# A mixture-of-experts kernel on Trainium2: a quarter of the last expert's second down tile moved from SyncE's queue to GpSimd's, in four strips of eight partitions

## The chip, the cores and the metric

The kernel runs on one core of one Trainium2 chip. The metric is device time in microseconds of one execution; the kernel before takes 1707.98 us (median of 3 runs, 1707.73 to 1708.21).

## The reference

The kernel computes a two-layer transformer block stack and then a second block whose last part is a mixture-of-experts feed-forward. Only that last part matters here: 272 tokens of width 1024, 16 experts, each of which takes its 34 best tokens (2 * 272 / 16).

```python
logits = jnp.einsum('ld,de->le', hs, w_router)
aff = jax.nn.softmax(logits, axis=-1)
g, idx = lax.top_k(aff.T, cap)
xg = hs[idx]
a = jnp.einsum('ecd,edf->ecf', xg, w_gate)
u = jnp.einsum('ecd,edf->ecf', xg, w_up)
y = jnp.einsum('ecf,efd->ecd', jax.nn.silu(a) * u, w_down)
y = y * g[..., None]
out = jnp.zeros((L, D)).at[idx.reshape(-1)].add(y.reshape(-1, D))
```

The result is added to the stream, normalised (RMS) and the last 256 tokens are the output. All weights are float32. An expert has a gate and an up matrix of 1024 x 2048 and a down matrix of 2048 x 1024: 24 MB, read once from device memory.

## The kernel before, in words

All five engines run one straight program each; semaphores tie them together. Weights come through a ring of six places of 2 MB (`RING_T`: 128 partitions of 4096 float32, that is 16 KB a partition). `LOADS` lists the tiles in the order in which they take the places; SyncE (SP) walks that order and issues one transfer a tile, or one of 4 MB for two neighbouring places (`pair_ring`, L3423). Before a transfer SP waits on `w.prev.left`, the semaphore that TensorE raises when it has left the tile that lay in that place before. The transfer raises the semaphore of the place (`w.sem`) by 16 when all of it has landed.

An expert `e` has twelve tiles: `("g", e, i)`, `("u", e, i)` and `("d", e, i)` for i = 0 to 3. TensorE (PE) takes them in `gate_up(e, i)` (the matmuls of L1417 and L1418, gate into partitions 0 to 33 of a PSUM bank, up into 64 to 97) and `down(e, i, u)` (L1444 and L1445, four steps `c` of 128 rows of the down matrix each, left and right half of the output). Each step shows as two rows a line, so `down` of a tile has eight rows of L1444. Between them `turn_hidden` transposes the hidden values (L1429).

The last expert (e = 15) is cut finer, so that its last tiles can be used while they arrive. In SP's order its last tiles are: `("g", 15, 3)` (L3420), `("u", 15, 3)` in two halves (L3452), `("d", 15, 0)` and `("d", 15, 1)` whole (L3420), `("d", 15, 2)` in two halves and `("d", 15, 3)` in four quarters (L3463). PE waits for the whole of `("d", 15, 1)` on `w.sem`; for the pieces of the last two tiles it waits on `last0` to `last5`.

After the last matmul of `down` ScalarE and VectorE copy the expert's output (L3146), PE adds it to the stream (L1480), the norm follows on VectorE and ScalarE (L3152 to L3176, L2199 to L2212), and SP stores the output in four transfers (L3467, L3469).

GpSimd (POOL) has 39 instructions in the whole program. Its part in the experts is `pool_experts` (L3267 on): two memsets, one of `Y`, one of `OG`, and three multiplications that weigh the one-hot routing map. After them its program ends. It issues no transfer. `WK`, which the change writes to, is a scratch tile of the routing that nobody reads after the first expert.

Of the kernel before, what the change touches and what calls it, by code (L numbers as in the profile page):

```python
# [20 lines left out]
SLOT = 4096  # L21
# [3 lines left out]
E_N = 16  # L25
# [76 lines left out]
PIECES["d", 0, 0] = (0, 2, 4, 8)  # L102
PIECES_OF = {y: len(PIECES[x]) - 1 for tiles, x in REFILLS for y in tiles}
PIECES_OF.update({("g", 0, 2): 4, ("u", 0, 2): 4})

BESIDE = {("g", 1, 3): 3, ("u", 1, 3): 2, ("d", 1, 0): 4}
BESIDE.update({("g", 2, 1): 3, ("u", 2, 1): 2, ("g", 2, 2): 4, ("g", 3, 0): 3, ("u", 3, 0): 2, ("g", 3, 1): 4})
# [182 lines left out]
def bc(ap, *shape):  # L290
# [15 lines left out]

    "split_hi", "split_lo", "dhh", "dhl", "rooted", "rooted_t", "cxs", "lam_d", "dcos", "drope", "amax", "asoft", "osq", "osub", "onorm", "czero", "conv",

    "routed", "sel", "wkzero", "rscaled", "rmax", "rexp", "raff", "rtop", "rmask", "rank", "above", "onehot", "ogzero", "og", "yzero", "esilu", "edown", "fin_in", "fin_rs", "fin_root", "weighed", "final_d", "final_a",
]  # L310


# [968 lines left out]
def pe_experts(nc, k):  # L1281
# [150 lines left out]
    def down(e, i, u):  # L1432
        w = k.weight_at("d", e, i)
        pieces = e == E_N - 1 and i >= 2
        if not pieces:
            pe.wait_ge(w.sem, w.n)
        t = P["eturn", e, i]
        pe.wait_ge(t.taken, t.done)
        for c in range(4):
            if pieces and (i == 3 or c % 2 == 0):  # L1440
                pe.wait_ge(s[f"last{c // 2 if i == 2 else 2 + c}"], 16)
            hs = v.HD[e % 2][:, 4 * i + c, :]
            first, end = i == 0 and c == 0, i == 3 and c == 3
            pe.matmul(u.t[0:CAP, :], hs, w.v(4, 1024)[:, c, 0:512], start=first, stop=end)  # L1444
            ins = pe.matmul(u.t[64:64 + CAP, :], hs, w.v(4, 1024)[:, c, 512:1024], start=first, stop=end)  # L1445
            if 2 * c + 2 in PIECES.get(("d", e, i), ())[1:-1]:
                ins.then_inc(s["first_used"], 1)
        if i < 3:
            ins.then_inc(s["edown"], 1)
            w.left = (s["edown"], 3 * e + i + 1)  # L1450
        else:
            ins.then_inc(u.full, 1)
            w.left = (u.full, u.n)
# [1814 lines left out]
def pool_experts(nc, k):  # L3268
    pool, s, v, P = nc.gpsimd, k.sem, k.ex, k.banks
    pool.wait_ge(P["rms", "ffn2"].full, P["rms", "ffn2"].n)  # L3270
    pool.memset(v.WK[0:16, 0:6], 2.0).then_inc(s["wkzero"], 1)
    pool.memset(v.mx, 0.0).then_inc(s["wkzero"], 1)

    u = P["egu", 0, 3]
    pool.wait_ge(u.full, u.n)
    pool.memset(v.Y[32:64, :, :], 0.0).then_inc(s["yzero"], 1)
    pool.wait_ge(s["yzero"], 1)
    pool.memset(v.OG.rearrange("p a b -> p (a b)"), 0.0).then_inc(s["ogzero"], 1)
    pool.wait_ge(s["onehot"], 6)
    pool.wait_ge(s["ogzero"], 1)  # L3280
    for i, (r, m) in enumerate(TILES):
        o = v.OH[0:m, i, :].rearrange("p (e s) -> p e s", s=CAP)
        af = v.AFF[0:m, i, :].rearrange("p (e a) -> p e a", a=1).to_broadcast([m, E_N, CAP])
        pool.tensor_tensor(v.OG[0:m, i, :].rearrange("p (e s) -> p e s", s=64)[:, :, 0:CAP], o, af, ALU.mult).then_inc(s["og"], 1)


def gpsimd_program(nc, k):
# [17 lines left out]
def sync_program(nc, k):  # L3305
    sp, s, A, P = nc.sync, k.sem, k.A, k.banks
# [58 lines left out]
    def part(x, e, i):  # L3365

        if x == "d":
            return A["w_down_2"][e, i // 2][:, SLOT * (i % 2):SLOT * (i % 2 + 1)]
        return A["w_gate_up_2"][e, i][:, SLOT * (x == "u"):SLOT * (x == "u") + SLOT]
# [52 lines left out]
    def pair_ring(x, e, i):  # L3422

        head, tail = k.ring[x, e, i], k.ring[("u", e, i) if x == "g" else ("d", e, i + 1)]
        sp.wait_ge(*head.prev.left)
        sp.wait_ge(*tail.prev.left)
        src = A["w_gate_up_2"][e, i] if x == "g" else A["w_down_2"][e, i // 2]
        sp.dma_start(flat(k.ring.pair((x, e, i))), src).then_inc(head.sem, 16)

    heads = set(PAIRED.values())  # L3430
    for e in range(E_N):
        if e:
            for i in range(4):
                for x in "gu":
                    if (x, e, i) in heads:
                        pair_ring(x, e, i)
                    elif (x, e, i) in PAIRED:
                        continue
                    elif (x, e, i) not in PIECES_OF and (x, e, i) != ("u", E_N - 1, 3):
                        beside_ring(x, e, i)  # L3440
        if e == 5:

            sp.wait_ge(*k.first["g", 3, 0].left)
            sp.dma_start(k.CB[:, :], A["fin"].broadcast_to([128, D])).then_inc(s["fin_in"], 16)
        if e == E_N - 1:


            w = k.ring["u", e, 3]
            sp.wait_ge(*w.prev.left)
            for c in range(2):  # L3450
                a, b = 2 * D * c, 2 * D * (c + 1)
                sp.dma_start(w.t[:, a:b], part("u", e, 3)[:, a:b]).then_inc(s[f"lastu{c}"], 16)  # L3452
        for i in range(4):
            if ("d", e, i) in heads:
                pair_ring("d", e, i)
            elif e and (e < E_N - 1 or i < 2) and ("d", e, i) not in PIECES_OF and ("d", e, i) not in PAIRED:
                beside_ring("d", e, i)
    for i, n, first in ((2, 2, 0), (3, 4, 2)):
# [131 lines left out]
```

## Time and profile before

| | us |
|---|---|
| median of 3 runs | 1707.98 |
| the profiled execution's own time | 1706.41 |
| its span, first to last instruction | 1704.7 |
| TensorE busy | 1608.2 (94%) |
| VectorE busy | 734.9 (43%) |
| ScalarE busy | 472.3 (28%) |
| GpSimd busy | 33.6 (2%) |

The profile is of one execution. TensorE's granted clock is 0.98 of full speed over the span. In the experts' part, from about 870 us on, the 16 DMA engines are busy throughout and move some 432 GB/s. The chain of work that ended last has PE in 70% of the span and DMA in 25%. The profiled execution's own time is 1.7 us above its span.

### The profile page before, as it was taken

The numbers are of one execution on the slowest core, as the hardware profiler recorded it, in microseconds if no ns is written. First come the engines' busy times: TensorE is split into PE (matmuls) and PEld (weight loads), VectorE is DVE, ScalarE is ACT, GpSimd is POOL, SyncE is SP. The second block draws the span as 40 slices with busy tenths as digits, with TensorE's granted clock in tenths as the row PEclk, the third lists the DMA queues.
The fourth block names the chain that finished last, engine by engine and source line by source line (L and its number), as shares of the span: only waits on it lengthen the run. The fifth ranks groups of instructions, "written<-read, shape, count | busy, mean of one in ns | idle before, by whom it ended". The sixth has DMA issues, their size and how long they took to land.

```text
span 1704.7 us, 22917 instructions
## 1 busy us (share of the span) xinstructions
PE 1608.2 (94%) x9593; PEld 980.0 (57%) x9593; DVE 734.9 (43%) x1462; ACT 472.3 (28%) x839; POOL 33.6 (2%) x39
## 2 busy tenths in 40 slices
PE   7999999999999999999999989889889889889998
PEld 5777999998999999787322322323223223223332
DVE  3778888878886557885111101101101101111102
ACT  3537634348653337743000000000000000000001
POOL 0100000000000001100100000000000000000000
PEclk9999999999999999999999999999999999999999
DMA  9964479891466454249999999999999999999997
GB/s 390 374 245 194 187 308 355 322 356 60 189 255 227 170 219 152 107 169 384 421 399 431 430 436 432 431 433 432 432 433 431 432 432 431 434 433 431 431 428 298
DMA packets 37972, 577.69 MB, mean 339 GB/s; under 512 B 4304, under 2 KB 5360, under 8 KB 9584
## 3 DMA queue, kind: packets, MB, share of 16 engines
q1 hardware_dynamic: 37872, 576.24, 81.7%
q8 instruction: 77, 1.26, 0.3%
q14 instruction: 23, 0.19, 0.0%
HBM read 575.17 MB, written 1.05 MB: 338 GB/s over the span
## 4 chain that ended last, share of the span: by engine, by line
PE 70%; DMA 25%; DVE 2%; issue 1%; ACT 1%; SPq 0%; DVEq 0%; ACTq 0%
DMA RING_T<-in_w_gate_up 23%; PE P L1417 17%; PE P L1444 6%; PE P L991 5%; PE P L993 5%; PE P L992 5%; PE P L595 4%; PE P L1009 2%; PE P L1008 2%; PE P L1010 2%; PE P L604 2%; PE P L1375 1%; DMA RING_T<-in_w_down 1%; PE P L1179 1%; PE P L1181 1%
## 5 line engine op out<-in xcount | busy, mean ns | idle before, releaser
L1417 PE MATMUL P<-RING_T,SCR 128*34 128x512 f32 x928 | 429.5, 618 | 62.4 <-DMA RING_T<-in_w_gate_up 57.2
L1418 PE MATMUL P<-RING_T,SCR 128*34 128x512 f32 x960 | 444.5, 618 | 0.0
L1417 PEld LDWEIGHTS P<-RING_T,SCR 128*34 128x34 f32 x928 | 102.5, 115 | 337.1 <-issue 317.3
L3105 DVE TENSOR_TENSOR SCR<-P,SCR 34x512 f32<-34x512 f32 x64 | 44.4, 693 | 500.6 <-ACT SCR L2169 500.5
L1444 PE MATMUL P<-RING_T,SCR 128*34 128x512 f32 x480 | 222.0, 612 | 14.9 <-issue 14.0
L1445 PE MATMUL P<-RING_T,SCR 128*34 128x512 f32 x480 | 222.3, 612 | 0.0
L2169 ACT ACTIVATE SCR<-P 34x512 f32<-34x512 f32 x64 | 37.6, 588 | 543.7 <-PE P L1418 543.7
L993 PE MATMUL P<-SCF 128*128 128x256 f32 x640 | 181.1, 283 | 0.0
L991 PE MATMUL P<-SCF 128*128 128x256 f32 x640 | 181.1, 283 | 0.0
L992 PE MATMUL P<-SCF 128*128 128x256 f32 x640 | 181.1, 283 | 0.0
L1444 PEld LDWEIGHTS P<-RING_T,SCR 128*34 128x34 f32 x480 | 51.2, 114 | 148.7 <-issue 144.2
L991 PEld LDWEIGHTS P<-SCF 128*128 128x128 f32 x640 | 122.9, 192 | 0.0
L993 PEld LDWEIGHTS P<-SCF 128*128 128x128 f32 x640 | 122.9, 192 | 0.0
L992 PEld LDWEIGHTS P<-SCF 128*128 128x128 f32 x640 | 122.9, 192 | 0.0
L2654 DVE TENSOR_TENSOR SCF<-RING_T,SCF 128x1024 fp32r<-128x1024 f32 x88 | 106.1, 1221 | 30.0 <-ACT SCF L1818 30.0
L1818 ACT ACTIVATE SCF<-RING_T 128x1024 fp32r<-128x1024 f32 x88 | 91.9, 1054 | 52.7 <-PE P L1010 27.9
L1418 PEld LDWEIGHTS P<-RING_T,SCR 128*34 128x34 f32 x960 | 106.0, 115 | 0.0
L1540 ACT ACTIVATE SCR<-P 128x256 f32<-128x256 f32 (+7 forms) x112 | 45.1, 417 | 199.5 <-PE P L1375 125.5
L1008 PE MATMUL P<-SCF 128*128 128x256 f32 x352 | 99.6, 283 | 0.0
L1009 PE MATMUL P<-SCF 128*128 128x256 f32 x352 | 99.6, 283 | 0.0
L1010 PE MATMUL P<-SCF 128*128 128x256 f32 x352 | 99.6, 283 | 0.0
L2327 DVE SCALAR_TENSOR_TENSOR RING_T<-RING_T,CB 128x1024 f32<-128x1024 f32 x80 | 93.1, 1220 | 9.0 <-DMA RING_T<-in_ada_w 4.8
(465 smaller groups left out, 2533.4 us busy)
## 6 DMA issues: line engine op xcount, KB each, us to landing
RING_T<-in_w_gate_up SPq DMA_DIRECT2D x47, 4096.0 KB, 20.5
RING_T<-in_w_down SPq DMA_DIRECT2D x22, 4096.0 KB, 21.6
RING_T<-in_ada_w SPq DMA_DIRECT2D x24, 2048.0 KB, 10.6
RING_T<-in_ffn_w SPq DMA_DIRECT2D x22, 2048.0 KB, 8.1
RING_T<-in_w_gate_up SPq DMA_DIRECT2D x15, 2048.0 KB, 19.0
RING_T<-in_ffn_w SPq DMA_DIRECT2D x22, 1024.0 KB, 6.6
RING_T<-in_w_down SPq DMA_DIRECT2D x11, 2048.0 KB, 18.4
RING_T<-in_ab_w_in SPq DMA_DIRECT2D x7, 2048.0 KB, 17.0
```

The lines of the kernel that those rows point to most:

```text
L991: pe.matmul(o, wh, v.HH[:, 0, c, :], start=c == 0, stop=False)
L992: pe.matmul(o, wh, v.HH[:, 1, c, :], start=False, stop=False)
L993: ins = pe.matmul(o, wl, v.HH[:, 0, c, :], start=False, stop=c == KC - 1)
L1008: pe.matmul(o, wh, v.HR[:, f % NHD, 0, :], start=f == 0 and m % 2 == 0, stop=False, skip_group_check=True)
L1009: pe.matmul(o, wh, v.HR[:, f % NHD, 1, :], start=False, stop=False, skip_group_check=True)
L1010: ins = pe.matmul(o, wl, v.HR[:, f % NHD, 0, :], start=False, stop=f == 21, skip_group_check=True)
L1417: pe.matmul(u.t[0:CAP, :], xs, wg.v(KC, 512)[:, c, :], start=c == 0, stop=c == KC - 1)
L1418: ins = pe.matmul(u.t[64:64 + CAP, :], xs, wu.v(KC, 512)[:, c, :], start=c == 0, stop=c == KC - 1)
L1444: pe.matmul(u.t[0:CAP, :], hs, w.v(4, 1024)[:, c, 0:512], start=first, stop=end)
L1445: ins = pe.matmul(u.t[64:64 + CAP, :], hs, w.v(4, 1024)[:, c, 512:1024], start=first, stop=end)
L2327: nc.vector.scalar_tensor_tensor(out=src, in0=src, scalar=1.0, in1=k.CB[:, :], op0=ALU.mult, op1=ALU.mult, accum_out=k.MOD[:, layer, 4 * i ...
L2654: nc.vector.tensor_tensor(lo, w.up()[:, :, z, j * 128:(j + 1) * 128], hi.bitcast(F32), ALU.subtract).then_inc(k.sem["lo"], 1)
```

## The change

One tile, `("d", 15, 1)`, is named `SHARED`. SP loads its partitions 0 to 95 as before. GpSimd, at the end of its program, waits for the same semaphore value as SP (`w.prev.left`), and then issues eight transfers: four times a tiny one (8 partitions of 8 float32 from the `c_cols` input into the scratch tile `WK`; nobody waits for it) and behind it eight partitions of the tile, every fourth one: 96, 100, ... 124, then 97, 101, ... 125, and so on. Each of these strips is 8 x 16 KB = 128 KB. PE waits for both the place's semaphore and for `shared` at 64 (four transfers of 16).

```diff
+SHARED = ("d", E_N - 1, 1)
...
+        if ("d", e, i) == SHARED:
+            pe.wait_ge(s["shared"], 64)
...
+    w, src = k.ring[SHARED], k.A["w_down_2"][SHARED[1], 0][:, SLOT:2 * SLOT]
+    pool.wait_ge(*w.prev.left)
+    for r in range(96, 100):
+        pool.dma_start(v.WK[0:8, 8 * (r - 96):8 * (r - 96) + 8], k.A["c_cols"][0:8, :]).then_inc(s["spare"], 16)
+        pool.dma_start(w.t[r:128:4, :], src[r:128:4, :]).then_inc(s["shared"], 16)
...
+            elif ("d", e, i) == SHARED:
+                w = k.ring[SHARED]
+                sp.wait_ge(*w.prev.left)
+                sp.dma_start(w.t[0:96, :], part("d", e, i)[0:96, :]).then_inc(w.sem, 16)
```

How it moves instructions, first on SP, at the end of the last expert. Before (`in_w_down` is the down matrix, `full4` and `full0` are raised by PE at the end of a `gate_up`):

```order
L3420 DMA RING_T<-in_w_gate_up 128x4096 [waits full1]
L3452 DMA RING_T<-in_w_gate_up 128x2048 [waits full1]
L3452 DMA RING_T<-in_w_gate_up 128x2048
L3420 DMA RING_T<-in_w_down 128x4096 [waits full4] x2
L3463 DMA RING_T<-in_w_down 128x2048 [waits full0]
L3463 DMA RING_T<-in_w_down 128x2048
```

And after the change, the same place:

```order
L3428 DMA RING_T<-in_w_gate_up 128x4096 [waits full1]
L3460 DMA RING_T<-in_w_gate_up 128x2048 [waits full1]
L3460 DMA RING_T<-in_w_gate_up 128x2048
L3428 DMA RING_T<-in_w_down 128x4096 [waits full4]
L3467 DMA RING_T<-in_w_down 96x4096 [waits full4]
L3475 DMA RING_T<-in_w_down 128x2048 [waits full0]
L3475 DMA RING_T<-in_w_down 128x2048
```

The second whole down tile has become one of 96 partitions; nothing else moved on SP.

On POOL, the end of its program after the change (before, it ends with the three multiplications):

```order
L3287 TENSOR_TENSOR SCR<-SCR 16x16x34
L3291 DMA SCR<-in_c_cols 8x8 [waits full4]
L3292 DMA RING_T<-in_w_down 8x4096
L3291 DMA SCR<-in_c_cols 8x8
L3292 DMA RING_T<-in_w_down 8x4096
L3291 DMA SCR<-in_c_cols 8x8
L3292 DMA RING_T<-in_w_down 8x4096
L3291 DMA SCR<-in_c_cols 8x8
L3292 DMA RING_T<-in_w_down 8x4096
```

Eight transfers stand behind one wait; nothing of POOL's is queued behind them.

On PE, the start of `down(15, 1)` after the change (before, the same row as L1444 waits for `taken1` and `weights3` alone):

```order
L1430 MATMUL P<-C,SCR 128x34 [waits taken4,taken1]
L1430 MATMUL P<-C,SCR 128x34 x3
L1447 MATMUL P<-RING_T,SCR 34x512 [waits taken1,shared,weights3]
L1448 MATMUL P<-RING_T,SCR 34x512
L1447 MATMUL P<-RING_T,SCR 34x512
```

One wait is added, in front of all the rest of PE's program.

## Rows read from the trace of the kernel before

**Rows 1.** The page: DMA busy and GB/s in 40 slices, and the chain by engine.

```profile
DMA  9964479891466454249999999999999999999997
GB/s 390 374 245 194 187 308 355 322 356 60 189 255 227 170 219 152 107 169 384 421 399 431 430 436 432 431 433 432 432 433 431 432 432 431 434 433 431 431 428 298
...
PE 70%; DMA 25%; DVE 2%; issue 1%; ACT 1%; SPq 0%; DVEq 0%; ACTq 0%
```

**Rows 2.** Chain that ended last, last 24 us: start us, us, what.

```profile
1670.40 0.39 PE P L1417
...
1673.13 19.89 DMA RING_T<-in_w_down
1693.02 0.04 issue
1693.06 0.62 PE P L1444
```

**Rows 3.** Stretches: length, busy of PE, PEld, DVE, ACT, POOL; PEclk; DMA share, GB/s.

```profile
1400.00:1600.00 200.00, 180.45 (x864) 60.09 (x864) 29.79 (x76) 12.64 (x24) 0.00 (x0) 0.96 1.00 432
...
1660.00:1685.00 25.00, 24.29 (x130) 8.83 (x128) 3.28 (x7) 3.05 (x4) 0.00 (x0) 1.00 0.99 421
...
1688.00:1689.00 1.00, 1.00 (x8) 0.35 (x6) 0.00 (x0) 0.00 (x0) 0.00 (x0) 1.00 0.52 213
1689.00:1690.00 1.00, 1.00 (x6) 0.24 (x4) 0.00 (x0) 0.00 (x0) 0.00 (x0) 1.00 0.50 205
1690.00:1691.00 1.00, 1.00 (x8) 0.34 (x6) 0.00 (x0) 0.00 (x0) 0.00 (x0) 1.00 0.40 164
1691.00:1692.00 1.00, 1.00 (x8) 0.16 (x6) 0.00 (x0) 0.00 (x0) 0.00 (x0) 1.00 0.27 111
1692.00:1693.00 1.00, 0.88 (x4) 0.00 (x0) 0.00 (x0) 0.00 (x0) 0.00 (x0) 1.00 0.15 53
```

**Rows 4.** Timeline of SP, last issues of weights: start us, us of issuing, line.

```profile
1652.82 0.91 SPq L3452 DMA_DIRECT2D RING_T<-in_w_gate_up  x2
1661.41 1.57 SPq L3420 DMA_DIRECT2D RING_T<-in_w_down  x2
1670.86 2.70 SPq L3463 DMA_DIRECT2D RING_T<-in_w_down  x6
```

**Rows 5.** Source L3420 from 1650 us (one gate, two down tiles): start and landing.

```profile
L3420 SPq DMA_DIRECT2D RING_T<-in_w_down x2: 328/760/1193, 1661.4 to 1661.8; - x2
...
DMA to landing us min/median/max: 16.0/16.8/21.3
```

**Rows 6.** Timeline of PE at the two whole down tiles.

```profile
1678.48 0.62 PE L1444 MATMUL P<-RING_T,SCR 128*34 128x512 f32 x1
...
1682.04 0.43 PE L1429 MATMUL P<-C,SCR 34*128 34x34 f32 x4
1683.14 0.62 PE L1444 MATMUL P<-RING_T,SCR 128*34 128x512 f32 x1 [0.67 <-DMA RING_T<-in_w_down]
```

**Rows 7.** Timeline of PE at the last step.

```profile
1692.28 0.59 PE L1444 MATMUL P<-RING_T,SCR 128*34 128x512 f32 x1
...
1693.06 0.62 PE L1444 MATMUL P<-RING_T,SCR 128*34 128x512 f32 x1 [0.18 <-DMA RING_T<-in_w_down]
```

**Rows 8.** Issues by line: KB each, median us from issue to landing.

```profile
RING_T<-in_w_down SPq DMA_DIRECT2D x2, 256.0 KB, 3.6
...
SCR<-in_c_cols SPq DMA_DIRECT2D x1, 4.0 KB, 1.6
```

**Rows 9.** Groups of instructions of POOL: busy us, mean ns of one.

```profile
L3278 POOL MEMSET SCR<- 128x3072 f32 x1 | 2.7, 2657 | 0.1
```

More of the change, by code:

```diff
@@ L307 @@
     "split_hi", "split_lo", "dhh", "dhl", "rooted", "rooted_t", "cxs", "lam_d", "dcos", "drope", "amax", "asoft", "osq", "osub", "onorm", "czero", "conv",
-    "routed", "sel", "wkzero", "rscaled", "rmax", "rexp", "raff", "rtop", "rmask", "rank", "above", "onehot", "ogzero", "og", "yzero", "esilu", "edown", "fin_in", "fin_rs", "fin_root", "weighed", "final_d", "final_a",
+    "routed", "sel", "wkzero", "rscaled", "rmax", "rexp", "raff", "rtop", "rmask", "rank", "above", "spare", "shared", "onehot", "ogzero", "og", "yzero", "esilu", "edown", "fin_in", "fin_rs", "fin_root", "weighed", "final_d", "final_a",
 ]
```

## The prediction

> **What bounds the kernel now.** I read the page first: from about 870 us on the DMA engines show 9 tenths in every slice and the rate stands at 431 to 436 GB/s [rows 1]. The chain of work is 70% PE and 25% DMA [rows 1], so the end of the experts' part is set by the stream of weights, with PE close behind. The chain's last pieces say who ends last: PE up to 1670.8 us, SP's six issues, then one transfer of 19.89 us that lands at 1693.02, and PE's last step from 1693.06 [rows 2]. Behind that step stand 1704.7 - 1693.06 = 11.6 us (copy, add, norm, store) that the change leaves alone.
>
> The stretches tell how the stream ends. Over 200 us the 16 engines move 432 GB/s at a share of 1.00 [rows 3]: 27.0 GB/s each, so one partition's row of 16,384 B takes an engine 0.607 us, and a tile of 128 rows is eight rows or 4.86 us an engine. But the engines do not finish together. From 1688 on the share is 0.52, 0.50, 0.40, 0.27, 0.15 [rows 3]: about half of them are done by 1688, and the others trail by 2 to 5 us. The work left after 1688 is 0.52 + 0.50 + 0.40 + 0.27 + 0.15 = 1.84 us of all 16 engines. Spread evenly it would end at 1689.8 and not at 1693.0. So there are up to 3.2 us in balancing the engines, and that is the whole stake of this change as a gain: 0.19% of the time. **A measurement of this kernel can tell some 0.2% (3.4 us) from no change.**
>
> How close PE is behind: `down(15, 0)` starts at 1678.48, its transposes end at 1682.47, and `down(15, 1)` starts at 1683.14 after 0.67 us of waiting [rows 6]. The last step waits only 0.18 us of idle by the profile, and its matmul follows the one before, which started at 1692.28, by 0.78 instead of the usual 0.43 us [rows 7]: some 0.35 us of waiting. So PE could end at most 0.67 + 0.35 = 1.02 us sooner, if weights came early enough from `("d", 15, 0)` on.
>
> **The change, part by part.**
>
> SP's transfer of the tile: 96 rows in place of 128, six rows an engine in place of eight. Each engine has 2 x 0.607 = 1.21 us less from SP. SP still issues one transfer, at 0.33 to 1.19 us [rows 5]; nothing gained or lost there, as the queue of the engines is 16.8 to 21.3 us deep at that time [rows 5] and hides it.
>
> GpSimd's four strips: 32 rows. The bytes are the same, so all engines together have the same 128 rows. What counts is on which engines the strips fall. A strip has eight rows of 16 KB, so it can keep at most eight engines busy with a row each. The trace of before has no transfer of eight partitions and no transfer from POOL, so I bound it from both sides. If the strips fall evenly, each engine gets 2 rows back: 0. If all four fall on the same eight engines, these have 6 + 4 = 10 rows (+1.21 us) and the other eight have 6 (-1.21 us). The Trainium skill ("DMA: Bandwidth & Descriptors", on why a DMA increments its semaphore by 16) says that GpSimd's transfer of eight rows takes eight engines that follow each other from a cursor that moves on; by that the tiny one takes one half and the strip always the other half, and the result would be one of the two outer values, never 0. No row here shows it.
>
> - On the eight engines that trail: their last landing moves from 1693.02 to 1694.23. The strips are issued from 1661.4 on and share the engines with what SP has queued, so up to 4 x 0.607 = 2.43 us are put ahead of `("d", 15, 0)`, which landed at 1661.41 + 16.8 = 1678.2 [rows 4, 5] and would land at 1680.6. PE starts there at 1680.7. From there PE needs 1682.47 - 1678.48 = 3.99 us to be ready for tile 1, and 1692.28 + 0.43 - 1683.14 = 9.57 us to the last step: 1694.26, when the last piece lands too. The last step starts at 1694.28 in place of 1693.06: **+1.2 us**.
> - On the eight that lead: they end at 1688 + 1.2 = 1689.2, still ahead of the rest. The trailing ones end at 1691.8. Tile 1 was issued at 1661.8, took 21.3 us [rows 5] and so landed at 1683.1; now it lands at 1681.9, before PE is ready. PE runs through from 1678.48: + 3.99 + 9.57 = 1692.04 for the last step, in place of 1693.06: **-1.0 us**.
>
> The tiny transfers: 8 x 32 B each. The nearest row is the transfer of 4 KB that lands in 1.6 us [rows 8]; its bytes are nothing to an engine (4 KB is a quarter of one 16 KB row, 0.15 us at most if all on one). Four of them: 0 to 0.6 us on one engine. I take 0, by the bytes.
>
> GpSimd's issuing: eight instructions behind a wait that ends with SP's, at 1661.4 [rows 4]. Nobody's work is queued behind them on POOL. It matters only if the last strip lands after PE wants it. That is 1683.1 before, and PE could be late to tile 1 by 0.35 us without moving the end. There is no row of an issue on POOL. Lower bound: SP's 0.33 us [rows 5], in all 2.6 us. Upper bound: POOL's longest instruction, 2.66 us [rows 9], in all 21.3 us. The strip itself needs about the 3.6 us of a transfer of 256 KB [rows 8]. Last strip landed: 1667.6 to 1686.3. I take the lower half, since issuing a transfer is no pass over 3072 elements a partition: inside the cover of 21.7 us, price 0, and +2.8 us at the upper end (1686.3 - 1683.1 - 0.35). VectorE is busy 3.28 us of the 25 us from 1660 to 1685 [rows 3]. If it held GpSimd up for all of it, that would still be inside the cover for any issue up to 1.8 us. The Trainium skill ("SBUF — State Buffer", on who interferes with whom) says that some VectorE operations lock GpSimd out while it writes the descriptors of a transfer; by that the strips come up to those 3.3 us later.
>
> PE's second wait: no instruction of its own in the order; if the strips are there, 0.
>
> **Sum and choice.** -1.0, 0 or +1.2 us by the place of the strips, and 0 to +2.8 from issuing. Nothing in the trace says which half trails. I take the trailing half (+1.2), for a reason of the bounds: everything else that the change adds (eight issues, four more transfers, one more wait, two queues that take turns on one engine) can only cost. The profiled execution took 1706.41 us, 1.57 below the median of 1707.98; 1706.41 + 1.2 = 1707.6 for such an execution, and against the median 1707.98 + 1.2 = **1709.2 us**.
>
> **The rivals.**
>
> *The strips fall on the leading half.* For it: the tail shows that half of the engines are free from 1688 [rows 3], and the four strips and tiny ones between them look made to pick one half. Against it: no row names the halves. Time: 1707.98 - 1.0 = 1707.0. Chance 0.30.
>
> *The strips bring no shift at all:* each falls on other engines, or what ends the stream is not the engine but the place in SBUF that it writes to, which has the same rows to take whoever brings them. For it: a share of 1.00 at 27.0 GB/s each [rows 3] fits both limits. Time: 1708.0. Chance 0.20.
>
> *GpSimd is late, and I am on the wrong side of 0.2%.* Mechanism: PE stands at `down(15, 1)` for the strips. It decides from the point at which the last strip lands after 1683.5; each us beyond is a us at the end. For +3.4 us the last strip must land at 1686.9, that is (1686.9 - 3.6 - 1661.4) / 8 = 2.7 us an issue. At 3.5 us an issue: 1661.4 + 28 + 3.6 = 1693.0, PE then has 9.57 us to the last step: 1702.6, +9.5 us, 1717.5. For it: GpSimd has issued no transfer before, and its first one may be slow. Against it: only its own longest instruction is as slow. Chance 0.10.
>
> The forecast (trailing half) has 0.40.
>
> **How the numbers follow.** The first three cases lie within 1707.0 to 1709.2, all closer to before than 3.4 us, together 0.90. The forecast case with issues at the upper bound would come to 1709.2 + 2.8 = 1712.0. Executions of before differ by 0.5 us among three. The range must hold 8 in 10: from 1706.4 (leading half, less the spread) to 1711.4 (trailing half, strips a little late). Faster by over 0.2% would need more than the whole stake of 3.2 us: 0.03. Slower by over 0.2%: nearly all of the late GpSimd, 0.09. Within: 0.88.
>
> **What would show it.** The stretches from 1688 on: if the trailing half got the strips, the shares after 1688 fall to zero one to one and a half us later than now and the lead ends about 1687; if the leading half, the 0.5 comes later and the zero sooner, near 1692. The timeline of PE at tile 1: a wait for `in_w_down` from POOL longer than 0.67 us would be the late GpSimd; no wait at all the leading half. In the issues by line, four transfers of 128 KB on POOL landing well before 1683 confirm the cover. I am wrong if the end moves by more than 3.4 us, if the stretches after 1688 look as before, or if something before 1661 us changes, where the change does nothing.

## The result, and the profile after

| | before | after |
|---|---|---|
| median of 4 runs each, same chip | 1707.95 us (1707.73 to 1708.21) | 1721.29 us (1719.24 to 1724.83) |
| profiled execution, its span | 1706.41 us, 1704.7 us | 1722.38 us, 1720.8 us |

The change makes the kernel slower: ratio 1.0083, 95% interval 1.0072 to 1.0095, or 13.3 us. The prediction said 1709.2 us, within 1706.4 to 1711.4. A few executions took 300 us or more longer, whatever the kernel (one of before at 2003.6 us, one of a variant at 3226.0 us), and the ratios leave them out.

The page of the changed kernel, DMA busy and GB/s in 40 slices, and the chain by engine, as [rows 1] of before:

```profile
DMA  9864479881566463349999999999999999999996
GB/s 392 356 246 198 186 309 362 319 345 54 215 232 237 152 247 147 119 180 395 415 402 430 433 433 433 431 433 431 434 430 435 432 430 430 433 431 431 433 396 183
...
PE 65%; DMA 30%; DVE 2%; issue 1%; ACT 1%; SPq 0%; DVEq 0%; ACTq 0%
```

The slices end with 396 and 183 in place of 428 and 298, and five per cent of the chain have gone from PE to DMA. The chain of before ended with a wait for SP's last piece [rows 2]. Here its last wait is the one for SP's 96 partitions of the cut tile: 36.22 us of DMA, up to 1699.54, and behind it PE runs through the rest of `down` without a wait. First the timelines of SP and POOL and the issues by line, then PE at the two whole down tiles, as [rows 4, 6, 8]:

```profile
1662.94 0.33 SPq L3428 DMA_DIRECT2D RING_T<-in_w_down  x1
1663.32 1.14 SPq L3467 DMA_DIRECT2D RING_T<-in_w_down  x1
1672.61 2.72 SPq L3475 DMA_DIRECT2D RING_T<-in_w_down  x6
```

```profile
1663.22 0.70 POOL L3291 DMA_DIRECT2D SCR<-in_c_cols  x1 [825.89 <-PE P L1419]
1663.91 0.52 POOL L3292 DMA_DIRECT2D RING_T<-in_w_down  x1
...
1666.98 0.52 POOL L3292 DMA_DIRECT2D RING_T<-in_w_down  x1
```

```profile
RING_T<-in_w_down SPq DMA_DIRECT2D x1, 1536.0 KB, 36.2
...
RING_T<-in_w_down POOLq DMA_DIRECT2D x4, 128.0 KB, 8.3
SCR<-in_c_cols POOLq DMA_DIRECT2D x4, 0.2 KB, 7.4
```

```profile
1685.30 0.43 PE L1430 MATMUL P<-C,SCR 34*128 34x34 f32 x4
1692.12 1.04 PE L1447 MATMUL P<-RING_T,SCR 128*34 128x512 f32 x1 [6.39 <-issue]
...
1698.46 0.43 PE L1430 MATMUL P<-C,SCR 34*128 34x34 f32 x4
1699.58 0.62 PE L1447 MATMUL P<-RING_T,SCR 128*34 128x512 f32 x1 [0.69 <-DMA RING_T<-in_w_down]
```

GpSimd is on time: eight issues of 0.52 to 0.70 us, and the strips land 8.3 us (median; 15.2 at most) after their issue, by 1666.98 + 15.2 = 1682.2 us. What is late is SP's own transfer of 96 partitions: it lands 36.2 us after its issue, at 1699.5, where the whole tile took 21.3 us [rows 5]. The tile ahead of it, `("d", 15, 0)`, is late too: PE stands 6.39 us for it, with the label "issue" since the profile names no releaser. The stretches say what the 16 engines did, as [rows 3]:

```profile
1400.00:1600.00 200.00, 180.69 (x868) 60.44 (x867) 28.95 (x74) 13.04 (x25) 0.00 (x0) 0.96 1.00 430
1660.00:1666.00 6.00, 5.74 (x38) 3.14 (x36) 0.99 (x2) 0.59 (x1) 2.78 (x6) 1.00 0.98 416
1666.00:1670.00 4.00, 4.00 (x22) 1.42 (x20) 0.00 (x0) 0.00 (x0) 1.50 (x3) 1.00 1.02 367
1670.00:1684.00 14.00, 10.33 (x45) 3.40 (x42) 0.99 (x2) 0.59 (x1) 0.00 (x0) 0.88 1.07 268
1684.00:1686.00 2.00, 1.73 (x12) 0.50 (x7) 0.00 (x0) 0.59 (x1) 0.00 (x0) 1.00 0.91 131
1686.00:1694.00 8.00, 1.88 (x6) 0.64 (x8) 0.99 (x2) 1.28 (x1) 0.00 (x0) 0.59 0.93 206
1694.00:1700.00 6.00, 5.31 (x20) 1.36 (x17) 0.30 (x1) 0.00 (x0) 0.00 (x0) 0.69 1.00 338
```

Read the last two columns together. From 1666 to 1694 the share stays between 0.91 and 1.07: in the mean the engines have a packet under way nearly all the time. Yet they move 367, 268, 131, 206 GB/s. Over these 28 us that is 4 x 367 + 14 x 268 + 2 x 131 + 8 x 206 = 7130, and 12,100 at 432: the missing 4970 are 11.5 us of the full stream. This execution is 1722.38 - 1706.41 = 16.0 us longer than the profiled one of before; 1.5 us of that were there before the change acts (SP issues the first down tile at 1662.94 and not at 1661.41), so 11.5 us stand against 14.5. The engines are not idle, their rows are slower: from 1670 to 1684 a row of 16,384 B takes 16 x 1.07 x 16,384 B / 268 GB/s = 1.05 us in the mean, in place of 0.607. That is what the experiments had to explain. PE's granted clock is 0.59 in the mean of 1686 to 1694, after PE has stood idle for 6.39 us, and its matmul at 1692.12 takes 1.04 us in place of 0.62. In this kernel that costs nothing, since PE then waits 0.69 us more for the tile that lands at 1699.5, and runs at full clock from there. In several of the experiments it does cost, and it is told there.

### The profile page after: what moved, and what is told of

Same layout as the page of the kernel before. It is cut to its first block, busy times and chain, and to the rows that moved or that the text cites. A ratio compares the mean times of both kernels' runs of the same rounds, so it can differ in the third digit from the quotient of the medians.

```text
span 1720.8 us, 22925 instructions
## 1 busy us (share of the span) xinstructions
PE 1603.4 (93%) x9593; PEld 982.1 (57%) x9593; DVE 734.8 (43%) x1462; ACT 472.4 (27%) x839; POOL 38.5 (2%) x47
## 3 DMA queue, kind: packets, MB, share of 16 engines
HBM read 575.17 MB, written 1.05 MB: 335 GB/s over the span
## 4 chain that ended last, share of the span: by engine, by line
PE 65%; DMA 30%; DVE 2%; issue 1%; ACT 1%; SPq 0%; DVEq 0%; ACTq 0%
DMA RING_T<-in_w_gate_up 28%; PE P L1418 14%; PE P L1447 5%; PE P L994 4%; PE P L992 4%; PE P L993 4%; PE P L596 4%; PE P L1010 2%; PE P L1009 2%; PE P L1011 2%; DMA RING_T<-in_w_down 2%; PE P L605 2%; PE P L1376 1%; PE P L1180 1%; PE P L1181 1%
## 5 line engine op out<-in xcount | busy, mean ns | idle before, releaser
L1418 PE MATMUL P<-RING_T,SCR 128*34 128x512 f32 x928 | 424.8, 612 | 67.6 <-DMA RING_T<-in_w_gate_up 63.9
```

The costliest lines, as they stand in the source:

```text
L1418: pe.matmul(u.t[0:CAP, :], xs, wg.v(KC, 512)[:, c, :], start=c == 0, stop=c == KC - 1)
```

## The experiments

All times of variants of the kernel stand beside runs of the kernel before on the same chip. The theories at the start, for where the loss comes from: the use of GpSimd's queue (A), the cut of the tile at partition 96 (B), the strips of eight rows (C). In the cuts of code, `...` stands for lines left out.

**1. The tiny transfers alone.** SP loads the whole tile, GpSimd issues only the tiny ones, PE waits for them.

```diff
-            pe.wait_ge(s["shared"], 64)
+            pe.wait_ge(s["spare"], 64)
...
-        pool.dma_start(w.t[r:128:4, :], src[r:128:4, :]).then_inc(s["shared"], 16)
...
-                sp.dma_start(w.t[0:96, :], part("d", e, i)[0:96, :]).then_inc(w.sem, 16)
+                sp.dma_start(w.t, part("d", e, i)[:, :]).then_inc(w.sem, 16)
```

> SyncE loads the whole second down tile again (128 partitions); GpSimd issues only the four tiny transfers behind the same wait, and TensorE waits for them at the second down tile. Theory A (the use of GpSimd's queue itself slows the engines): 1715 us or more, with GB/s under 320 in 1668 to 1695 us. Theory B (the cut of the tile over 96 partitions breaks the pairing of DMA engines and places in SBUF) and theory C (the strips of eight partitions share eight engines with SyncE's rows): 1708 us, stretches as before.

Measured: 1707.97 us beside 1707.59; ratio 1.0005 (0.9994 to 1.0016). A second queue, its issues and PE's second wait cost nothing that can be told.

**2. SP alone, 96 partitions and then 32.** Nothing on GpSimd: its wait and its eight transfers are left out, and PE waits for one transfer on `shared`.

```diff
                 sp.dma_start(w.t[0:96, :], part("d", e, i)[0:96, :]).then_inc(w.sem, 16)
+                sp.dma_start(w.t[96:128, :], part("d", e, i)[96:128, :]).then_inc(s["shared"], 16)
```

> No transfer from GpSimd. SyncE loads partitions 0 to 95 and then, in a transfer of its own, 96 to 127. Theory A and C: 1708 us (A: no second queue; C: no transfer of eight partitions). Theory B: 1714 us or more; the rate falls below 300 GB/s once the 96-partition transfer runs (from about 1678 us), and not before.

Measured: 1720.96 us, ratio 1.0081 (1.0052 to 1.0111), +13.4. A loss of the same size is there without any use of GpSimd; A falls, and C, which said 1708 us here, is not needed for it. Stretches of this kernel, and PE's start on the cut tile:

```profile
1666.00:1670.00 4.00, 4.00 (x22) 1.43 (x20) 0.00 (x0) 0.00 (x0) 0.00 (x0) 1.00 1.03 438
...
1672.00:1678.00 6.00, 6.00 (x30) 1.69 (x30) 0.99 (x2) 0.36 (x1) 0.00 (x0) 1.00 1.03 269
1678.00:1694.00 16.00, 8.36 (x30) 2.29 (x26) 1.29 (x3) 1.87 (x2) 0.00 (x0) 0.79 1.00 220
1694.00:1700.00 6.00, 4.26 (x11) 1.14 (x13) 0.00 (x0) 0.00 (x0) 0.00 (x0) 0.53 0.77 309
```

```profile
1695.74 1.03 PE L1447 MATMUL P<-RING_T,SCR 128*34 128x512 f32 x1 [3.75 <-issue]
```

The rate holds until 1672 us (418 GB/s from 1670 on), some 10 us after the cut tile's issue at 1661.7, and then falls to 269 and 220 GB/s. The fall comes 6 us sooner than expected.

Not all of this loss is the stream's. PE had stood idle for 5.63 and then 3.75 us before it started on the cut tile at 1695.74, its granted clock is 0.53 from 1694 to 1700, near the lower of its two levels (1.2 GHz), and seven steps of its matmuls take 5.7 us in place of 3.0 (0.82 to 0.86 us each for most of them, and not 0.43). PE has no wait behind that, so these 2.7 us go straight to the end. The profiled execution closes by this: the cut tile is started 1695.74 - 1683.14 [rows 6] = 12.6 us later than before, less the 0.35 us that PE waited at its last step [rows 7], plus 2.7, is 14.95; it took 1721.34 - 1706.41 = 14.93 us more. Experiments 3 and 4 have such slow steps too, 1.7 us each.

**3. SP alone, 96 partitions and the four strips.**

```diff
+                for r in range(96, 100):
+                    sp.dma_start(w.t[r:128:4, :], part("d", e, i)[r:128:4, :]).then_inc(s["shared"], 16)
```

> No transfer from GpSimd. SyncE loads partitions 0 to 95 and then the same four strips of eight partitions. Theory A: 1708 us. Theory B: as slow as the 96 and 32 cut. Theory C: slower than the 96 and 32 cut by the strips' 4 rows on eight engines, 1.2 to 2.4 us, and by more if sharing a place in SBUF is what costs.

Measured: 1718.66 us, ratio 1.0064 (1.0041 to 1.0088), +11.1: no worse than one transfer of 32. C had said 1.2 to 2.4 us slower than that, and was wrong here.

**4. GpSimd loads the 32 partitions in one transfer.**

```diff
+    pool.dma_start(w.t[96:128, :], src[96:128, :]).then_inc(s["shared"], 16)
```

> SyncE loads partitions 0 to 95, GpSimd 96 to 127 in one transfer of 32 partitions, two rows on each of 16 engines, none tiny. Theory A: as slow as the change, 1717 to 1725 us. Theory B: between 1714 and 1722 us. Theory C: 1708 to 1710 us, since all engines get two rows back and no eight of them get four.

Measured: 1721.39 us, ratio 1.0084 (1.0055 to 1.0113). Its stretches part the two pieces, since GpSimd's runs ahead of SP's queue:

```profile
1666.00:1670.00 4.00, 4.00 (x21) 1.33 (x18) 0.00 (x0) 0.00 (x0) 0.00 (x0) 1.00 1.06 223
...
1672.00:1678.00 6.00, 1.98 (x9) 0.72 (x10) 0.99 (x2) 0.59 (x1) 0.00 (x0) 0.86 1.03 422
1678.00:1694.00 16.00, 12.67 (x50) 3.67 (x46) 0.99 (x2) 1.87 (x2) 0.00 (x0) 0.84 1.00 218
```

Two dips at a full share, with 422 GB/s between them. By their order they belong to the 32 rows and then to the 96. C had said 1708 to 1710 us here. So after these four B stood, and C could no longer be the whole cause, only a part beside B. Next: what is it in the cut?

**5. The same quarter cut by columns.** The bytes on each queue are those of experiment 4.

```diff
-    pool.dma_start(w.t[96:128, :], src[96:128, :]).then_inc(s["shared"], 16)
+    pool.dma_start(w.t[:, 3072:4096], src[:, 3072:4096]).then_inc(s["shared"], 16)
...
-                sp.dma_start(w.t[0:96, :], part("d", e, i)[0:96, :]).then_inc(w.sem, 16)
+                sp.dma_start(w.t[:, 0:3072], part("d", e, i)[:, 0:3072]).then_inc(w.sem, 16)
```

> The same quarter of the tile goes to GpSimd's queue, cut by columns: SP loads columns 0 to 3071 of all 128 partitions, GpSimd the last 1024 columns of all 128 partitions in one transfer; TensorE waits for both. The bytes moved to the second queue are those of the change. Theory P (the cut over partitions is what costs): no row of the stream changes its place, so 1708 us, within 1 us of the kernel before. Rival (any cut of this tile between two transfers, or half a megabyte on a second queue in the middle of a full stream, upsets it): 1716 to 1722 us, as in all three kernels cut at partition 96.

Measured: 1708.13 us beside 1707.16, ratio 1.0004 (0.9995 to 1.0014). The rate holds in the stretch in which it fell in experiment 2 (and is 420 GB/s from 1678 to 1685):

```profile
1672.00:1678.00 6.00, 5.72 (x28) 2.09 (x30) 0.43 (x2) 0.00 (x0) 0.00 (x0) 1.00 1.00 425
```

So neither the split nor the second queue costs anything that can be told, only the partitions left out.

**6. Transfers alone, by shape.** A kernel that leaves all of the computation out and writes loaded weights to the output. A group is eight transfers like the first line, then SP waits for all of them.

```python
    for j in range(8):
        sp.dma_start(B[0:96, j, :], src(j)[0:96]).then_inc(done, 16)
    settle()
```

> Not the reference's computation: transfers alone, all other engines idle. SP issues ten groups of eight back-to-back transfers into eight places of one tensor and waits for each whole group. Rows of 16 KB unless said: 128 partitions; 128 partitions of 12 KB; partitions 0 to 95; 0 to 63; 32 to 95; 96 to 127; eight partitions 4 apart; 128 and 0 to 95 in turn; 0 to 95 from another tensor whose rows lie 16 KB apart, not 32; 16 to 111. Theory P (places in SBUF: in a transfer of 128 partitions no two engines share a way into SBUF, in every other cut several may): 128 partitions at about 430 GB/s (39 and 29 us); 0 to 95 has 64 rows behind half of the ways, so 39 us in place of 29 or more; 0 to 63 at about 215 GB/s (39 us in place of 20), 32 to 95 near 430 (20 us), 96 to 127 about 215 (20 us); the tensor read from makes no difference; 128 and 96 in turn are slower than the mean of the two. Rival H (reads from HBM, rows 32 KB apart): the tensor with rows 16 KB apart runs otherwise, and 0 to 63 runs like 32 to 95, which read the same rows. Rival S (a cut costs nothing by itself, only in a full stream with skewed engines): every group at about 430 GB/s, or as far below as a fixed start of 2 to 4 us per group makes it; only the in-turn group shows the loss.

The timeline of SP gives each group's start (L3501: 128 partitions of 12 KB rows; L3504: 0 to 95; L3507: 0 to 63; L3510: 32 to 95; L3513: 96 to 127; L3520 on: in turn; L3525: the other tensor; L3528: 16 to 111):

```profile
42.42 3.94 SPq L3501 DMA_DIRECT2D B<-in_w_down  x8
74.34 3.96 SPq L3504 DMA_DIRECT2D B<-in_w_down  x8
130.58 5.05 SPq L3507 DMA_DIRECT2D B<-in_w_down  x8
173.68 5.04 SPq L3510 DMA_DIRECT2D B<-in_w_down  x8
195.84 3.59 SPq L3513 DMA_DIRECT2D B<-in_w_down  x8
...
227.16 0.36 SPq L3520 DMA_DIRECT2D B<-in_w_down  x1
...
276.46 3.80 SPq L3525 DMA_DIRECT2D B<-in_ada_w  x8
334.16 4.32 SPq L3528 DMA_DIRECT2D B<-in_w_down  x8
390.86 0.84 SPq L3533 DMA_DIRECT2D out<-B  x2
```

Stretches inside of the groups, in the same order from 128 partitions of 16 KB on (POOL only beside them):

```profile
22.00:32.00 10.00, 0.00 (x0) 1.00 1.03 441
...
54.00:64.00 10.00, 0.00 (x0) 1.00 1.01 431
...
90.00:110.00 20.00, 0.00 (x0) 1.00 1.01 235
...
135.00:155.00 20.00, 0.00 (x0) 1.00 1.01 206
...
176.00:186.00 10.00, 0.00 (x0) 1.00 0.99 423
...
198.00:210.00 12.00, 0.00 (x0) 1.00 1.06 217
```

By differences of the starts: 1.5 MB eight times takes 31.9 us over 128 partitions and 56.2 us over 96. 1 MB eight times takes 43.1 us into partitions 0 to 63 and 22.2 us into 32 to 95, though both read the same rows. From the tensor with rows 16 KB apart it is 57.7 us, into 16 to 111 it is 56.7 us. So it is the place written to: H (reading from device memory) falls, and S (a cut costs nothing by itself) with it. In all the stretches shown the share is about 1. 0 to 95 was expected at 39 us or more and takes 56.2: more than the counting of places gives. That engines meet at a place and hold each other up there is a reading; the profile does not name the engine of a row or its way into SBUF. Eight strips of eight partitions (L3516, 1 MB in all) took 227.16 - 218.28 = 8.9 us, 147 GB/s at a share of 0.43; 5.46 us of that were SP's issuing. One expectation was wrong: in turn with whole tiles (49.3 us) the cut one costs what it costs alone (the mean of 41.7 and 56.2 is 48.9).

The Trainium skill ("SBUF — State Buffer", "Door 1: The DMA port swizzle") says that the DMA engines reach SBUF by 16 ports, and that bits 4 to 2 and bit 6 of the partition's number choose one. By that 0 to 63 and 96 to 127 reach 8 of them, 32 to 95 all 16; the trace agrees, at 206, 217 and 423 GB/s. Worked out from the same rule, as an estimate, 96 rows, 64 of them behind eight ports, would need 4/3 of the balanced time; that disagrees with 56.2 against 31.9 us, 1.76 times, and the measurement decides.

**7 and 8. Place alone, in the kernel.** The tile is whole, and a transfer of 64 rows goes ahead of it into a free place; the twins differ in one pair of numbers (`-` is the first, `+` the second).

```diff
-                sp.dma_start(k.ex.EX[2][0:64, :], k.A["w_down_2"][SHARED[1], 0][0:64, SLOT:2 * SLOT]).then_inc(s["shared"], 16)
+                sp.dma_start(k.ex.EX[2][32:96, :], k.A["w_down_2"][SHARED[1], 0][0:64, SLOT:2 * SLOT]).then_inc(s["shared"], 16)
```

> The tile is loaded whole as in the kernel before, and nothing goes through GpSimd. One more transfer of SP's queue ahead of it: 64 rows of 16 KB (1 MB) into partitions 0 to 63 of a place that no one uses any more; TensorE waits for it where it waits for the tile. Its bytes alone are 2.4 us at the stream's rate, so 1710.4 us if its partitions made no difference. Theory P (partitions 0 to 63 lie behind half of the ways into SBUF): at least 2.6 us more than its twin into 32 to 95, so 1713 us, and some 5 us more again if the lag of half of the engines grows while it passes, 1718. Rival (any transfer of fewer than 128 partitions, or reading the rows from HBM): the same time as its twin.

> Twin of the one into partitions 0 to 63: the same 64 rows are read, at the same place in the queue, and written to partitions 32 to 95, which bench_shapes ran at 423 to 445 GB/s. Theory P: only its bytes, 2.4 us, so 1710.4 us, within 1 us. Rival (any transfer of fewer than 128 partitions upsets the stream): as slow as its twin, 1713 to 1720 us.

Measured beside 1706.74 us: into 0 to 63 1720.56 us, ratio 1.0079 (1.0064 to 1.0094); into 32 to 95 1710.61 us, ratio 1.0023 (1.0013 to 1.0033). The same bytes at the same point of the queue differ by 10.0 us by the partitions they go to (+13.8 and +3.9; the bytes alone are 2.4). Some 2.1 us of the 10.0 are PE's clock: in the slow twin PE starts on the tile at 1694.96 after 4.87 us of idling, its granted clock is 0.58 from 1695 to 1700, five steps take 4.25 us in place of 2.15, and no wait follows. In the other PE waits 0.22 us for the last piece, so a slow clock before it costs nothing. Stretches of the two, the slow one first:

```profile
1675.00:1680.00 5.00, 3.64 (x20) 1.03 (x16) 0.99 (x2) 1.66 (x2) 0.00 (x0) 1.00 0.99 216
1680.00:1685.00 5.00, 1.67 (x4) 0.44 (x6) 0.00 (x0) 0.21 (x1) 0.00 (x0) 0.71 1.05 213
```

```profile
1675.00:1680.00 5.00, 5.00 (x28) 1.46 (x26) 0.99 (x2) 1.87 (x2) 0.00 (x0) 1.00 1.00 426
1680.00:1685.00 5.00, 1.96 (x12) 0.56 (x8) 0.30 (x1) 0.00 (x0) 0.00 (x0) 1.00 0.99 421
```

And PE's start on the tile in the slow one:

```profile
1694.96 1.07 PE L1447 MATMUL P<-RING_T,SCR 128*34 128x512 f32 x1 [4.87 <-DMA RING_T<-in_w_down]
```

**9. Does the lag between engines matter?** Alone, 0 to 63 costs (43.1 - 22.2) / 8 = 2.6 us more than 32 to 95; in the kernel 10.0, or some 8 without PE's clock. There, half of the engines seem to be late [rows 3]. So, transfers alone again: nine in a row, the fifth one changed, with and without a preface that is meant to load one set of eight engines. In the code `full(a, b)` loads whole tiles, `rows(a, b)` partitions a to b - 1, and `skew` is the preface.

```python
    skew(True)
    full(0, 4)
    rows(0, 96)
    full(5, 9)
    end()
```

> Not the reference's computation: transfers alone. Every group is nine transfers of SP, four of 128 partitions (2 MB, 4.9 us each by bench_shapes), a middle one, four of 128; the middle one is 128 partitions, or 0 to 95, or 0 to 95 followed by 96 to 127 as its own. Each of the three comes with the engines in step, and behind a preface that gives one set of eight engines 8 packets of 16 KB more than the other (about 5 us behind), and behind the same preface with the other set late; then 32 to 95 and 0 to 63 behind the first preface. Theory L (places in SBUF, and the lag of half of the engines makes it cost more than in step): in step 0 to 95 costs 1.8 us more than 128 partitions and 96 + 32 costs 4.3 us more (6.65 and 2.6 against 4.9, by bench_shapes); behind a preface at least 3 us more than that, up to the 13 us of the real kernel, and the 16 landings end further apart than the 5 us they had; 32 to 95 costs no more than its bytes (2.4 us less than 128 partitions), 0 to 63 at least 2.6 us more than that. Rival (the lag plays no part, the rest of the 13 us comes from elsewhere in the kernel): the same 1.8 and 4.3 us behind a preface as in step, within 1 us.

The group starts are SP's first issues at 0.73, 47.20, 95.70, 146.66, 210.56, 279.84, 352.42, 416.52, 486.46, 559.90, 620.38 and the store at 689.08; two of them:

```profile
146.66 0.34 SPq L3514 DMA_DIRECT2D B<-in_w_down  x1
210.56 0.29 SPq L3514 DMA_DIRECT2D B<-in_w_down  x1
```

| group | in step | first preface | other preface |
|---|---|---|---|
| nine whole tiles | 46.5 | 63.9 | 64.1 |
| fifth one 0 to 95 | 48.5 (+2.0) | 69.3 (+5.4) | 69.9 (+5.8) |
| fifth one 0 to 95, then 96 to 127 | 51.0 (+4.5) | 72.6 (+8.7) | 73.4 (+9.3) |
| fifth one 32 to 95 | | 60.5 (-3.4) | |
| fifth one 0 to 63 | | 68.7 (+4.8) | |

The same cut costs 3.4 to 4.8 us more behind either preface; each group ran once. The preface itself took 17.4 us, not 5. By the rule of ports that the Trainium skill gives (see experiment 6), its eight adjacent partitions reach only two. SP's own issues stood there as well (nine over 16.84 us), though the last was out more than 40 us before the group's end. So the lag may have been larger than the kernel's 5 us, and this shows a direction, not the kernel's sum.

**10. The strips alone, in the kernel.** Whole tile by SP; the change's tiny ones and strips into a free place.

```diff
-        pool.dma_start(w.t[r:128:4, :], src[r:128:4, :]).then_inc(s["shared"], 16)
+        pool.dma_start(k.ex.EX[2][r:128:4, :], src[r:128:4, :]).then_inc(s["shared"], 16)
```

> The tile is loaded whole by SP as before; GpSimd issues the change's four tiny transfers and four strips of eight partitions, but into a place that no one uses any more, and TensorE waits for them as in the change. So only the strips are added, the cut at partition 96 is not made. Theory P: eight partitions 4 apart lie behind eight different ways into SBUF, so the strips cost their own bytes only, 4 rows of 16 KB on each of eight engines: between 0 (leading set) and 2.4 us (trailing set), 1707.5 to 1710.5 us. Rival (the strips are a good part of the 13 us): 1713 us or more.

Measured: 1713.34 us beside 1706.66, ratio 1.0039 (1.0023 to 1.0054), +6.7. That is what the rival said (1713 or more) and not what P said (at most 1710.5), by 0.3 us only, with executions from 1710.8 to 1714.3. The rate is 309 GB/s from 1666 to 1670 and 336 from 1670 to 1684, at shares of 1.07 and 1.00. So strips of eight rows cost more than their bytes as well. By the rule of ports that the Trainium skill gives (see experiment 6), no two of the eight partitions share one.

**11 and 12. The change's idea without its cut.** SP takes 3072 columns of all partitions, sixteen strips of 4 KB rows take the rest, each behind a tiny one, or, in the twin, ahead of it.

```diff
+    for r in range(16):
+        p = r % 4 + 32 * (r // 4)
+        pool.dma_start(v.WK[0:8, 8 * r:8 * r + 8], k.A["c_cols"][0:8, :]).then_inc(s["spare"], 16)
+        pool.dma_start(w.t[p:p + 29:4, 3072:4096], src[p:p + 29:4, 3072:4096]).then_inc(s["shared"], 16)
```

> What the change meant, without cutting SP's transfer over partitions: SP loads columns 0 to 3071 of all 128 partitions, GpSimd the last 1024 columns in sixteen transfers of eight partitions 4 apart (rows of 4 KB), each behind a tiny one, so that all sixteen fall on the same eight DMA engines. By the arithmetic of the prediction's middle term, with an even row price: every engine is spared 8 rows of 4 KB (1.2 us), eight engines get them back twice (2.4 us), so eight engines are 1.2 us earlier and eight 1.2 us later. If the set is the trailing one, 1709.2 us; if it is the leading one, 1706.8; its twin then shows the other. If strips of eight partitions cost by themselves as the cut at 96 does: over 1712 for both.

> Twin of the kernel with the tiny transfer ahead: the tiny one stands behind each of the sixteen strips, so the strips fall on the other eight DMA engines. By the same arithmetic the twin's time mirrored around that of the kernel before: 1706.8 us where the twin is 1709.2, or the reverse, 2.4 us between the two at most, less by what 2 us of the lag that the other engines have. If neither differs from the kernel before by more than 0.5 us, the assignment of engines does not follow the tiny transfers, or varies from run to run.

> The kernel of tiny_behind again, unchanged: its first profile was of an execution of 3.2 ms and says nothing. Its 31 issues on GpSimd's queue end before the wait of 12.4 us that the 32nd met in tiny_ahead. If the strips of 4 KB rows cost by where they lie, the DMA rate falls below 400 GB/s while its share stays near 1, about from 1668 to 1690 us, and the last landing is some 8 us late. If instead GpSimd's queue is what is late, the rate stays at 416 GB/s or more and TensorE waits at the second down tile for a strip that was issued late or landed long after its issue.

Measured beside 1706.66: 1719.0 us, ratio 1.0076 (1.0063 to 1.0088), and 1715.41 us, ratio 1.0053 (1.0039 to 1.0067). A second series of the twin, beside 1707.22, took 1715.15 us, ratio 1.0047 (1.0031 to 1.0063); its profile is the one shown. Neither is near the 1706.8 or 1709.2 us that the arithmetic of engines gave. POOL's last issue in the first, and PE's timeline at the second tile in the twin:

```profile
1690.62 0.52 POOL L3293 DMA_DIRECT2D RING_T<-in_w_down  x1 [12.38 <-issue]
```

```profile
1681.80 0.43 PE L1430 MATMUL P<-C,SCR 34*128 34x34 f32 x4
1689.80 1.04 PE L1447 MATMUL P<-RING_T,SCR 128*34 128x512 f32 x1 [7.57 <-issue]
```

Here it is GpSimd's queue that is late. In the first, the 32nd issue stood 12.38 us and its strip landed some 4 us later, at about 1694.7; in the twin the last strip was issued at 1675.75 and took up to 14.0 us, to 1689.7. The prediction's rule for this (each us beyond 1683.5 is a us at the end) gives +11.2 and +6.2 us. It lacks PE's clock: after 11.14 and 7.57 us of idling PE's first five steps take 3.57 and 3.67 us in place of 2.15, at a granted clock of 0.73 and 0.71 in the mean of the 5 us from 1695 and from 1690 on. That adds 1.4 and 1.5 us, in all 12.6 and 7.7; the profiled executions took 12.5 and 7.65 us more than that of before. The rate stayed at 407 GB/s or more until 1680 in the twin and fell to 338 and 308 in the ten us after. So these two say nothing of the 1.2 us either way that balancing was to bring: that is still untested.

**13. The second queue's 0.5 MB, priced in step.** Nine whole tiles on SP; GpSimd adds a quarter tile once the first has landed.

```python
    stream()
    ahead()
    pool.dma_start(B[96:128, 9, :], src(0)[96:128]).then_inc(side, 16)
    end(1)
```

> Not the reference's computation: transfers alone, engines in step. Every group is nine transfers of SP of 128 partitions (46.5 us by bench_skew), and once the first has landed GpSimd adds 0.5 MB from its own queue: nothing; the last 1024 columns of 128 partitions; partitions 96 to 127; four strips of eight partitions 4 apart, each behind a tiny transfer (as in the change); the four strips each ahead of a tiny one; the four strips alone; 2048 columns of partitions 32 to 95. Theory P with full ways (in a full stream each way into SBUF is already kept full by one DMA engine, so a byte costs where its partition lies, whichever engine carries it, and more where two meet): 128 partitions and 32 to 95 cost their bytes spread over all, 1.2 us; 96 to 127 and all three strip groups put 4 rows of 16 KB behind each of eight ways, so at least 2.4 us, 3 to 6 us with what meeting costs, and the tiny transfers make little difference. Rival (a byte costs where its DMA engine is): strips on one set of eight engines 2.4 us, alone 1.2 us, 96 to 127 1.2 us.

First issues of the second and third group; the first is at 0.74, the others at 144.38, 197.19, 248.41 and 299.50, the store at 347.27:

```profile
47.23 0.33 SPq L3502 DMA_DIRECT2D B<-in_w_down  x1
94.96 0.33 SPq L3502 DMA_DIRECT2D B<-in_w_down  x1
```

| added by GpSimd | group, us | more than nothing |
|---|---|---|
| nothing | 46.5 | |
| 1024 columns of 128 partitions | 47.7 | +1.2 |
| partitions 96 to 127 | 49.4 | +2.9 |
| four strips, each behind a tiny one | 52.8 | +6.3 |
| four strips, each ahead of a tiny one | 51.2 | +4.7 |
| four strips alone | 51.1 | +4.6 |
| 2048 columns of 32 to 95 | 47.8 | +1.3 |

The groups stand in the order of the expectation; each ran once. The same half a megabyte costs 1.2 us where it is spread over all places and 2.9 to 6.3 us where it goes to partitions 96 to 127 only. The rival (a byte costs where its engine is) gave 1.2 for the rows that measured 2.9 and 4.6, and 2.4 for those that measured 4.7 and 6.3. The change's own pattern is the dearest, and 6.3 us in step agrees with the 6.7 us of experiment 10.

## Why the prediction was wrong

- **The bound.** Right: the stream of weights ends the kernel, PE close behind. The two kernels that kept the stream whole ended within 1 us of before (experiments 1 and 5), and 1 MB more at the full rate moved the end by 3.9 us (experiment 8), 2.4 of them its bytes. But the last wait moved: before it was for SP's last piece, now it is for the cut tile, and PE runs through behind it.
- **SP's 96 rows.** This is the step that failed: "Each engine has 2 x 0.607 = 1.21 us less from SP", and with it "The bytes are the same, so all engines together have the same 128 rows." It took 0.607 us a row from a stream in which every transfer has all 128 partitions, and carried it to another shape. In step, a transfer of partitions 0 to 95 takes 56.2 / 8 = 7.0 us in place of the 4 us of the same bytes over 128 (31.9 / 8), and beside whole tiles it costs 2.0 us more than a whole tile though it is a quarter smaller. Both bounds of an engine's work (-1.21 and +1.21 us) rested on the same price, so the range could not hold the result: it was 13.3 us, of which 1.2 had been forecast.
- **The four strips.** "If the strips fall evenly, each engine gets 2 rows back: 0", at the outside 1.21 us. Measured by themselves, with their bytes as an addition: 6.3 us in step, 6.7 in the kernel. If the tiny ones do move the strips to other engines, which no run shows, then that played a small part at most: ahead, behind or left out they differ by 1.7 us in one execution.
- **The rival "no shift at all"** had the mechanism in its hands, "the place in SBUF that it writes to", and drew the wrong conclusion from it, "which has the same rows to take whoever brings them". The place does count, but whoever brings the rows is not all that changes: the same bytes went at 206 GB/s into partitions 0 to 63 and at 423 into 32 to 95. A likely reading is that a whole tile gives each engine places of its own, and a cut one sends several to one place while others stand free; the rates fit it, no profile shows it. The kernel before has no row of that, and a row price without one is no upper bound: the range needed an open upper side.
- **GpSimd late.** The bound of 0.33 to 2.66 us an issue held, at 0.52 to 0.70, and the choice of its lower half was right. A strip's landing was taken at 3.6 us from another transfer and measured 8.3 in the median and 15.2 at most; the cover of 21.7 us hid that. The rival's rule for what lateness costs holds in experiments 11 and 12 once 1.4 and 1.5 us are added for PE's clock, which the prediction did not think of.
- **The tiny transfers and PE's second wait** at 0: right by experiment 1 (ratio 1.0005), for a stream that is otherwise whole; beside strips the tiny ones ahead may be worth up to 1.7 us (6.3 against 4.6, one execution).
- **SP's issue** of 1.14 us lies inside the bounds of [rows 5] and is hidden.

**How far the sum closes.** In step the parts are +2.0 for the cut at 96 and +6.3 for the strips: 8.3 of 13.3 us. Behind a preface the first is 5.4 to 5.8, which gives 11.7 to 12.1. But experiment 2 has no GpSimd and loses 13.4 us as well, where transfers alone lose 4.5 in step and 8.7 to 9.3 behind a preface. PE's clock is 2.7 us of that, which leaves 10.7, and some 1.4 to 2 us of experiment 2 stay unexplained. In the change itself the clock costs nothing, so the totals of the two are alike but not made of the same parts. Experiment 9 shows that a cut tile is dearer behind a preface; that this is the lag of some engines, and that the kernel's own lag is all of the rest, is argued, not shown.

## What to carry to other kernels

In a full stream of loads, cut a tile by columns and keep all 128 partitions in every transfer: a quarter by columns on another queue, in one transfer, was free (ratio 1.0004), a quarter by partitions cost 13 to 14 us. If a transfer must have fewer, 32 to 95 ran at full rate where 0 to 63 ran at half. When a late tile lets PE stand idle for several us, look at the granted clock behind the wait: where nothing is waited for afterwards, the slow steps are added to the delay. And when a row price is taken from the trace, ask which shape it belongs to: a share of 1.00 says that the engines have work, not that they go at their rate, so read share and GB/s together.

## What the hardware showed that was not expected

- 96 partitions are worse than the count of places gives: 235 GB/s, 1.76 times the time of the same bytes over 128, in step and with the other engines idle, and the loss is larger in the kernel's stream (13.4 us, 10.7 of them without PE's clock, against 4.5 for 96 and 32).
- Strips of eight partitions 4 apart cost 4.6 to 6.3 us for 0.5 MB beside a full stream that can take the same bytes in 1.2 us.
- GpSimd's queue takes an issue of eight rows in 0.52 us, but after 31 of them in 16 us the next stood 12.38 us, and a strip of 32 KB took up to 14.0 us to land.
- PE's granted clock is 1.00 behind the wait of 0.69 us in the changed kernel. Behind idle stretches of 3.75 to 11.14 us in experiments 2, 7, 11 and 12 it is 0.53 to 0.73 in the mean of the 5 or 6 us around the restart and behind it; 0.5 is the lower of its two levels (1.2 GHz). This took 2.7, 2.1, 1.4 and 1.5 us.
